# Hybrid diffusion step: a reordered opening, norm transposes at other places, and retention heads 1 to 3 written out

## What is computed

```python
def adaln(cvec, w, b):
    m = jax.nn.silu(cvec) @ w + b
    return jnp.split(m, N_MOD, axis=-1)      # shift, scale, gate; shift, scale, gate

def modulate(x, g, shift, scale):
    return rmsnorm(x, g) * (1.0 + scale) + shift

for l in range(DEPTH):
    mc, ml = adaln(c_ctx, ada_w[l], ada_b[l]), adaln(c, ada_w[l], ada_b[l])
    hc, hl = modulate(xc, norm_mix[l], ...), modulate(xl, norm_mix[l], ...)
    # l = 0: q, k, v, two gates = h @ weights; per head a forward and a backward scan over
    #        chunks of 128 tokens with decay exp(log_gamma * distance); y @ wo
    # l = 1: grouped-query attention, window 128, with a sink; y @ wo
    xc, xl = xc + mc[2] * yc, xl + ml[2] * yl
    hc, hl = modulate(xc, norm_ffn[l], ...), modulate(xl, norm_ffn[l], ...)
    # a = h @ w_in; depthwise conv of width 3; silu(g) * u; @ w_out
    xc, xl = xc + mc[5] * ffn(hc), xl + ml[5] * ffn(hl)
```

## Time and profile before

| | |
|---|---|
| median of 3 runs | 2097.97 us |
| the profiled execution, its whole time | 2103.55 us |
| its span, first to last instruction | 2101.7 us |
| mean granted TensorE clock | 0.985 |
| PE busy | 2016.7 us, 96% of the span |
| POOL, DVE, ACT busy | 752.6, 964.2, 662.9 us |
| DMA | 194.06 MB, mean 92 GB/s |

### The profile page before, as it was taken

One profiled execution on the slowest core, in us unless ns is written; L12 is line 12 of the kernel. 1 busy time (PEld: TensorE's weight loads), 2 busy tenths in 40 slices (PEclk: granted clock), 3 DMA queues, 4 the chain that ended last, 5 costly groups with the idle time before them and its releaser, 6 DMA issues.

```text
span 2101.7 us, 29771 instructions
## 1 busy us (share of the span) xinstructions
PE 2016.7 (96%) x11176; PEld 1680.7 (80%) x11176; DVE 964.2 (46%) x1281; ACT 662.9 (32%) x1323; POOL 752.6 (36%) x519
## 2 busy tenths in 40 slices
PE   6799999999999999999999999998979999999998
PEld 3685878588677847998898898895558998998996
DVE  2312420350133035753564475656624673575475
ACT  5332222222221234332233133425534332232232
POOL 3233233233323324433233333437844433333332
PEclk9999999999999999999999999998989999999999
DMA  7422332223223212342343222420002422222221
GB/s 296 177 71 70 102 118 71 77 93 102 77 91 110 70 50 98 113 150 70 120 140 111 70 73 77 171 78 16 1 11 91 151 72 79 70 80 73 77 71 51
DMA packets 53117, 194.06 MB, mean 92 GB/s; under 512 B 5920, under 2 KB 7328, under 8 KB 52000
## 3 DMA queue, kind: packets, MB, share of 16 engines
q1 hardware_dynamic: 48096, 174.68, 25.3%
q10 hardware_dynamic: 4928, 18.08, 2.2%
HBM read 185.65 MB, written 7.08 MB: 92 GB/s over the span
## 4 chain that ended last, share of the span: by engine, by line
PE 88%; issue 3%; ACT 3%; DVE 2%; POOL 2%; DMA 1%; DVEq 1%; POOLq 0%; ACTq 0%
PE ps L420 35%; PE ps L463 21%; PE ps L435 16%; PE ps L637 2%; PE ps L482 2%; PE ps L374 2%; PE ps L646 1%; ACT pr L1146 1%; PE ps L632 1%; POOL pr L1296 1%; PE ps L378 1%; PE ps L391 1%; PE ps L796 1%; PE ps L502 1%; PE ps L510 1%
## 5 line engine op out<-in xcount | busy, mean ns | idle before, releaser
L1190 POOL TENSOR_TENSOR w_l<-raw,w_h 128x1024 fp32r<-128x1024 f32 x232 | 564.7, 2436 | 1117.0 <-ACT w_h L845 1117.0
L420 PE MATMUL ps<-h_h,w_h 128*128 128x384 f32 (+1 forms) x1696 | 530.1, 313 | 2.7 <-issue 2.7
L420 PE MATMUL ps<-h_h,w_l 128*128 128x384 f32 (+1 forms) x1696 | 523.7, 309 | 0.0
L420 PE MATMUL ps<-h_l,w_h 128*128 128x384 f32 (+1 forms) x1696 | 523.6, 309 | 0.0
L845 ACT CAST w_h<-raw 128x1024 fp32r<-128x1024 f32 x232 | 245.3, 1059 | 559.0 <-PE ps L463 296.2
L420 PEld LDWEIGHTS ps<-h_h,w_h 128*128 128x128 f32 x1696 | 322.0, 190 | 16.2 <-issue 15.2
L420 PEld LDWEIGHTS ps<-h_l,w_h 128*128 128x128 f32 x1696 | 322.0, 190 | 2.6 <-issue 2.4
L420 PEld LDWEIGHTS ps<-h_h,w_l 128*128 128x128 f32 x1696 | 321.7, 190 | 0.0
L1562 DVE SCALAR_TENSOR_TENSOR cc<-ca,vec,cc 128x641 f32<-128x641 f32 x88 | 222.7, 2530 | 13.6 <-issue 12.4
L435 PE MATMUL ps<-w_h,h_h 128*128 128x512 f32 (+1 forms) x520 | 199.8, 384 | 1.0 <-issue 1.0
L435 PE MATMUL ps<-w_l,h_h 128*128 128x512 f32 (+1 forms) x520 | 198.2, 381 | 0.0
(11 more groups left out here) (190 smaller groups left out, 2670.9 us busy)
## 6 DMA issues: line engine op xcount, KB each, us to landing
raw<-stream_dram SPq DMA_DIRECT2D x312, 512.0 KB, 3.6
first_w<-first_dram SPq DMA_DIRECT2D x16, 512.0 KB, 15.6
gate<-gate_b_dram ACTq DMA_DIRECT2D x4, 1024.0 KB, 5.0
S<-state_dram ACTq DMA_DIRECT2D x4, 1024.0 KB, 7.4
new_state_dram<-st_out ACTq DMA_DIRECT2D x8, 512.0 KB, 3.1
xt<-x_dram ACTq DMA_DIRECT2D x5, 512.0 KB, 10.0
y_dram<-front SPq DMA_DIRECT2D x5, 512.0 KB, 2.6
rope_t<-rope_t_dram ACTq DMA_DIRECT2D x1, 512.0 KB, 9.1
```

The lines of the kernel that those rows point to most:

```text
L420: mm = nc.tensor.matmul(ps[:, banks + half, 0:width(half)], w, x[:, k, lo_hi(half)], start=(k == 0 and n == 0), stop=(k == KT - 1 and n == 2))
L1190: nc.gpsimd.tensor_tensor(w_l[:, r, :], raw[:, s, :], w_h[:, r, :].bitcast(F32), ALU.subtract).then_inc(raw_used[s], 1)
```

## The change

There are four edits.

1. **Small loads and the gate turn.** `gate` and the three table loads are issued from ACT in the middle of the opening, `rope_t` at its end without anything ahead of it. The exponentials move from ahead of the first evacuation to behind the evacuations of tiles 1 and 2; DVE's product with `tri` moves to behind the rotary work of q and k. DVE's wait for `rope_t` moves from ahead of the gate's copy to behind `gate_add`.
2. **Third modulation group.** `ada_first(2)` moves ahead of the transposes of token tiles 3 and 4, DVE's copy of it into the middle of `norm_f`, and the turns of groups 2 and 3 stand apart from their `ada_first`. `h_l` of token tile 4, half 0, is made by POOL.
3. **Norm transposes** in `first_tiles`: tile 3 after 2 steps k instead of 5, tile 4 after 6 instead of 8. Tile 4's second half of `norm_f` goes from ACT to DVE, its `h_l` half 0 from DVE to POOL, and ACT's `ada_copy` behind tile 3.
4. **Heads 1 to 3** are written out by a Python loop on the four engines. The condition in `hi` follows, since the head number is now a plain integer.

```diff
-POOL_LO = (0, 1, 3)
-            return t in (1, 3) if n == 0 else t >= 3 and hk == 1
+            return t in (1, 3) if n == 0 else (t, hk) == (3, 1)
+        def lo_on_pool(t, hk):
+            return t in (0, 1, 3) or (t, hk) == (4, 0)
@@ PE, first_tiles
-                first_pair(b, n, 0, range(0, 5))
+                first_pair(b, n, 0, range(0, 2))
                 norm_turn(n, 3)
-                first_pair(b, n, 0, range(5, KT))
+                first_pair(b, n, 0, range(2, 6))
                 norm_turn(n, 4)
+                first_pair(b, n, 0, range(6, KT))
@@ PE, opening
             ada_turn(0, 2)
+            ada_first(2)
             for t in range(3, TT):
                 norm_turn(0, t, (0,))
                 first_pair(b, 0, 0, range(0, 4))
-                ada_first(2)
-                first_pair(b, 0, 1, range(0, 2))
                 ada_turn(0, 3)
-                first_pair(b, 0, 1, range(2, 4))
+                first_pair(b, 0, 1, range(0, 1))
                 ada_first(3)
+                first_pair(b, 0, 1, range(1, 3))
                 ada_turn(0, 4)
+                first_pair(b, 0, 1, range(3, 4))
@@ PE, ACT, POOL, DVE
-            with pe.Fori(1, HEADS) as h:
+            for h in range(1, HEADS):
                 head(SEG["ret"], h, False)
@@ ACT, hi
-                if not (b.m0 + j < RING and isinstance(i, int)):
+                if not isinstance(i, int) or b.done(j, i) > RING:
@@ ACT, out_act
+                norm_f(n, 3, 1)
+                for hk in range(2):
+                    norm_hi(n, 3, hk)
                 ada_copy(SEG[NEXT_OF[n]], 0, 0, 3)
-                for t in (3, 4):
-                    norm_f(n, t, 1)
-                    for hk in range(2):
-                        norm_hi(n, t, hk)
+                for hk in range(2):
+                    norm_hi(n, 4, hk)
@@ ACT, opening and first head
                 if hk == 0:
                     hi(b0, 2, 0)
                     hi(b0, 3, 0)
-            act.dma_start(diff, dr["diff"]).then_inc(dec_in, 16)
-            ...
-            decay_tables(0)
-            decay_tables(1)
-            nc.scalar.activation(small[:, 56:64], small[:, 40:48], ACT.Exp, scale=float(P)).then_inc(dec_exp, 1)
-            act.dma_start(gate[:], dr["gate_b"][0]).then_inc(gate_in, 16)
+                    act.dma_start(gate[:], dr["gate_b"][0]).then_inc(gate_in, 16)
+                    act.dma_start(diff, dr["diff"]).then_inc(dec_in, 16)
+                    ...
             act.dma_start(rope_t[:], dr["rope_t"]).then_inc(rope_in, 16)
                     hi(b, j + RING, h)
+                    if first_head and j in (1, 2):
+                        decay_tables(j - 1)
@@ POOL, out_pool
                     norm_lo(n, 3, hk)
+                norm_lo(n, 4, 0)
@@ DVE, residual_norm
-                for hk in range(2):
-                    norm_lo(n, 4, hk)
+                norm_lo(n, 4, 1)
@@ DVE, opening and first head
             for t in range(TT):
                 norm_f(0, t, 0)
-            for t in (2, 4):
-                norm_lo(0, t, 0)
-            for n in range(2, 4):
-                ada_copy(None, n, 0, 0)
-                ada_mods(0, n + 1, FIRST[n])
+                if t == 2:
+                    ada_copy(None, 2, 0, 0)
+            norm_lo(0, 2, 0)
+            ada_mods(0, 3, FIRST[2])
+            ada_copy(None, 3, 0, 0)
+            ada_mods(0, 4, FIRST[3])
-                if first_head:
-                    dve.wait_ge(rope_in, 16)
                 ada_copy(b, 0, h, 0)
                     gate_add(0, adas + 1, 0, slice(0, 512))
+                if first_head:
+                    dve.wait_ge(rope_in, 16)
```

More of the change, by code:

```diff
@@ L312, in wait_lo @@
             for done, on_pool in ((hlo_pool, True), (hlo_dve, False)):
-                mine = [x for x in halves(n) if (x[0] in POOL_LO) == on_pool]
+                mine = [x for x in halves(n) if lo_on_pool(*x) == on_pool]
                 need = max((k + 1 for k, x in enumerate(mine) if x[0] in ts and x[1] == hk), default=0)
@@ L931, in decay_tables @@
             def decay_tables(d):
+                act.wait_ge(dec_lg, 1)
+                act.wait_ge(dec_in, 48)
                 for h in range(HEADS):
@@ L951, in _ @@
                     hi(b0, 3, 0)
-            act.dma_start(diff, dr["diff"]).then_inc(dec_in, 16)
[L953 to L956, removed]
-            decay_tables(0)
-            decay_tables(1)
-            nc.scalar.activation(small[:, 56:64], small[:, 40:48], ACT.Exp, scale=float(P)).then_inc(dec_exp, 1)
-            act.dma_start(gate[:], dr["gate_b"][0]).then_inc(gate_in, 16)
+                    act.dma_start(gate[:], dr["gate_b"][0]).then_inc(gate_in, 16)
+                    act.dma_start(diff, dr["diff"]).then_inc(dec_in, 16)
+                    act.dma_start(iota, dr["iota"]).then_inc(dec_in, 16)
+                    act.dma_start(tri, dr["tri"]).then_inc(dec_in, 16)
             act.dma_start(rope_t[:], dr["rope_t"]).then_inc(rope_in, 16)
@@ L974, in head @@
                     hi(b, j + RING, h)
+                    if first_head and j in (1, 2):
+                        decay_tables(j - 1)
+                    if first_head and j == 2:
+                        nc.scalar.activation(small[:, 56:64], small[:, 40:48], ACT.Exp,
+                                             scale=float(P)).then_inc(dec_exp, 1)
                     if j == 0:
@@ L1037, in _ @@
             head(b0, 0, True)
-            with act.Fori(1, HEADS) as h:
+            for h in range(1, HEADS):
                 head(SEG["ret"], h, False)
@@ L1266, in _ @@
                 lo(SEG["ret0"], j, 0)
-            for t in POOL_LO:
+            for t in (0, 1, 3, 4):
                 norm_lo(0, t, 0)
@@ L1270, in _ @@
                 lo(SEG["ret0"], j, 0)
-            for t in POOL_LO:
+            for t in (0, 1, 3):
                 norm_lo(0, t, 1)
@@ L1275, in _ @@
             rms(0)
-            with pool.Fori(1, HEADS) as h:
+            for h in range(1, HEADS):
                 for j in range(20):
@@ L1450, in _ @@
                 norm_lo(0, t, 1)
-            dve.wait_ge(dec_exp, 1)
-            for d in range(2):
-                op = V.tensor_tensor(dm[:, d], dm[:, d], over(tri[:, d, :], HEADS), ALU.mult)
-            op.then_inc(dec_ready, 1)
             gch = small[:, 56:64].rearrange("p (d h) -> p d h", d=2)
@@ L1487, in head @@
                     residual(h - 1, b, 4, h, 4)
+                if first_head:
+                    dve.wait_ge(dec_exp, 1)
+                    for d in range(2):
+                        op = V.tensor_tensor(dm[:, d], dm[:, d], over(tri[:, d, :], HEADS), ALU.mult)
+                    op.then_inc(dec_ready, 1)
+                    dve.drain()
                 ada_copy(b, 4, h, 1)
@@ L1533, in _ @@
             head(SEG["ret0"], 0, True)
-            with dve.Fori(1, HEADS) as h:
+            for h in range(1, HEADS):
                 head(SEG["ret"], h, False)
```

## The result

| | before | after |
|---|---|---|
| median of the paired runs | 2097.15 us (4 runs) | 2077.94 us (4 runs) |
| profiled execution, span | 2101.7 us | 2076.3 us |
| PE busy | 2016.7 us | 2010.2 us |
| mean granted clock | 0.985 | 0.988 |

The ratio is 0.9909, with a 95% interval of 0.9896 to 0.9922: the change takes off 19.2 us (16.4 to 21.8). I forecast 25.2. The two spans differ by 25.4 us, almost exactly the forecast. So the question for the experiments was why a sum that fits the two profiles misses the two medians by 6 us.

The account below looks back on a forecast made before the run. PE was busy 2016.7 of 2101.7 us, so gains come only from its gaps or half-speed matmuls. Opening 14.1 + heads 4.4 + layer openings 6.7 = 25.2 us, taken from the median 2097.97: 2072.8 us, range 2066 to 2083.

Parts of the forecast that it names:

- 6.7 in sum: Edit 3, three later layer openings: earlier first remainder and full clock save 2.9, 2.5 and 1.35 us.
- all four covers: Opening, edit 1: gate's load, weight tiles 2 and 3 (evacuations of tiles 0 and 1) and ACT's tables should not become late.
- 2.0 us of the clock: Gate turn, edit 1: behind a 0.8 us pause its four matmuls run at full speed, 1.72 us against 3.74.
- forecast of 10.9: Opening, edit 1: 8.9 us less wait at the gate turn plus 2.0 us from full clock.
- 3.2 forecast: Opening, edit 2: third group fills PE's 2.21 us pause at full speed; ACT's second-half norm_f starts near 45, not 48.22.
- rival of 2.2 us: Opening, edit 2: third group and transposes at half speed delay the pairs up to 2.2 us; within covers failing, 0.15.
- The new end: Layer openings, edit 3: POOL's three h_l at 1.25 us each end at 831.3 in n = 1, setting the first remainder.
- split as forecast: Three layer openings, edit 3: the pause ahead of part 1 splits, in sum 1 us.
- term of 4.4 us: Start of head 3, edit 4: written-out heads remove a 2.70 us issue gap and 1.69 us of slower first tile.
- an accident of the profiled execution: Rival, head 3's start: issue gap is accidental or returns elsewhere, edit 4 gives 0, result 2077.2 us; chance 0.07.
- Both jumps: Rival, starts of heads 2 and 3: both back jumps cost in timed runs, edit 4 worth 8.8 us, result 2068.4; chance 0.14.
- slower by instruction loads: Rival, heads 2 and 3: 14 more instruction loads each stall PE 4.4 us, cost 62, result 2139 us; chance 0.03.

Follow-up runs that it names:

- experiment 12: Changed kernel with the loop over heads 1 to 3 back on TensorE (PE) alone; other engines stay written out: 2081.14 us, ratio 0.9923 to the kernel before.
- experiment 1: The kernel before, unchanged, profiled and timed again: 2096.42 us, ratio 0.9998.
- experiments 5 and 9: Kernel before with edit 1 alone: 2091.91 us; with only edit 1's loads and tables reordered, DVE's wait for rope_t left ahead of the copy: 2090.52 us.
- experiment 7: Changed kernel with the third modulation group back at its old place (edits 1, 3, 4): 2082.97 us, ratio 0.9931 to the kernel before.
- experiments 2 and 12: 2: changed kernel with the loop over heads 1 to 3 back on all four engines (edits 1, 2, 3), 2082.84 us; 12: loop back on PE alone, 2081.14 us.
- experiment 10: Kernel before with the third modulation group at its new place (edit 2 alone): 2093.86 us, ratio 0.9984.

## Why the prediction came out as it did

The forecast was 2072.8, the result 2077.94: inside the range, 5.1 us too low. By places, each in all profiles that bear on it (start of one landmark on PE to the next; a layer opening is first norm transpose to gate turn; experiment 12 counts in the first two rows only):

| place | forecast | first pair | profiles without the edit | with it | difference |
|---|---|---|---|---|---|
| opening, to the scores of head 0 | 14.1 | 14.9 | 119.9 (4, 118.6 to 122.1) | 106.9 (4, 106.4 to 107.3) | 13.0 |
| three layer openings, each | 6.7 in sum | 6.4 | 29.1 (21, 28.5 to 30.2) | 27.4 (21, 27.3 to 27.7) | 1.66, 5.0 in sum |
| scores of head 2 to those of head 3 | 4.4 | 4.2 | 188.45 (8: five at 186.85, three at 191.0 to 191.2) | 187.0 (5) | 1.45 |
| scores of head 0 to those of head 2 | 0 | -0.4 | 373.75 (8) | 374.4 (5) | -0.6 |
| gate turn of n = 1 to the first transposes of n = 2 | 0 | 1.35 | 469.1 (8, 468.2 to 470.3) | 467.5 (5, 467.3 to 467.8) | 1.6 |

The sum is 13.0 + 5.0 + 1.45 - 0.6 + 1.6 = 20.4 us, against 19.2 measured (16.4 to 21.8). Two more stretches scatter over the fourteen profiles without a clear tie to an edit: from the scores of head 3 to the first transposes of n = 1 the first pair lost 3.35 us, from the gate turn of n = 2 to the transposes of n = 3 (266.4 to 269.1) it gained 2.1. With them, the first pair adds up to its 25.4.

**A gain that the prediction's sum lacks.** The last row of the table lies behind the heads, in the first FFN, and goes with edit 4: no profile with a loop on PE is as short as the longest of the five written out. The other matmuls of that stretch take 454.0 us in all fourteen profiles. The difference is in the seven `ada_block`, whose 16 matmuls use a weight chunk raw: their sum, each to the start of what follows, is 13.3 to 13.8 us written out and 14.2 to 16.5 else, with experiment 12 (loop on PE alone, 470.5 for the stretch) at the upper end. Two of the seven in the changed kernel, the same two in experiment 1, and the longest in experiment 12 (timelines of PE):

```profile
1028.06 1.92 PE L486 MATMUL ps<-raw,csil 128*32 128x512 f32 x16
1059.14 1.92 PE L486 MATMUL ps<-raw,csil 128*32 128x512 f32 x16
```

```profile
1042.74 2.20 PE L482 MATMUL ps<-raw,csil 128*32 128x512 f32 x16
1074.10 2.19 PE L482 MATMUL ps<-raw,csil 128*32 128x512 f32 x16
```

```profile
997.71 1.91 PE L487 MATMUL ps<-raw,csil 128*32 128x512 f32 x12
1000.43 1.05 PE L487 MATMUL ps<-raw,csil 128*32 128x512 f32 x4 [0.81 <-DMA raw<-stream_dram]
```

The last row names the chunk's load. Why it lands earlier where the heads are written out is not shown.

**Edit 1, right.** The wait was on `rope_t`, the copy follows in 0.84, and all four covers held: tile 2 starts at 59.48, no wait on `qk_evac` appears, `gate_add` and the tables cost nothing. The size went with the load: in the four profiles without edits 1 and 2 `rope_t` landed 9.1, 7.7, 6.8 and 6.7 us after its issue, and the pause was 9.69, 7.93, 6.61 and 6.60; issued ahead of the tables it landed in 3.4 to 3.6 us, in all eight profiles that have it so. The 2.0 us of the clock were 1.75 (from the gate turn to the scores of head 0 it is 50.90 in the first profile, 49.15 in the changed kernel): I took 3.74 from a timeline and 1.72 from the chain, and in a timeline the same four matmuls at full speed are 1.88. In two profiles (experiments 5 and 9) the opening is 8.0 us shorter (111.9); in a third without edit 2 (experiment 7, 108.78) it is 11.1, near the forecast of 10.9. Of the 3.1 us between them 1.5 are the half speed behind POOL's pause; before that, the first pairs ran at half speed for longer (`norm_f` of the second half at 47.15 and 46.94, against 45.45).

**Edit 2, right in place, too large.** 3.2 forecast, 2.0 and 1.9 in the profiles. I took full speed, "because the pause that would let the clock fall is the one that is filled"; that was the failed step of this term. The group's matmuls take 3.2 to 4.9 us in all six profiles with the edit, and there are two reasons. In four profiles (the changed kernel's two, experiments 2 and 12) PE is at the group at 25.1 to 25.8 us, before its weights: PE's weight loads wait 2.7 or 2.8 us for the chunks, and the clock falls meanwhile (granted 0.50 to 0.54 from 26.5 to 29.5 us in the first). In experiment 10 PE comes there at 29.5 and waits for no chunk, but all 16 run at half speed (1.06 us each and not 0.59), 3.64 us in sum. I had that as a rival of 2.2 us; it cost 1.3, as the pairs behind it run at full speed again. ACT's `norm_f` came 4.3 us earlier than in the profile before, but only 1.5 to 2.3 earlier (43.1 to 43.9) than in experiment 7. The rest goes with the clock: the second group took 3.64 us in the profile before, and 1.92 in the one after.

**Edit 3, right.** The new end is POOL's third `h_l`, 1.5 us behind ACT's cast of that tile, and the pauses are split as forecast, in sum 0.8 us in n = 1, 0.7 in n = 2 and 1.2 in n = 3. The gain per place has two parts: 1.15 us always (28.55 to 27.4), and 1.55 where the clock would have fallen, which it did in 7 of 21 places without the edit and in none of 21 with it. I counted the second part in two of three places, as the first profile had it.

**Edit 4 and the step that failed.** The term of 4.4 us was read rightly from the earlier trace rows, and it is in 3 of 8 profiles with loops and in 0 of 5 written out. In each of the three the page has 66 instruction packets, in the other five 57, and in the five written-out ones 70. So the gap comes in executions that load nine packets more, and three of them land around it. I still read it as code of the loop body that is loaded again, but that is argued: the view names no engine for these packets, though the prediction puts them on PE's queue. I had "an accident of the profiled execution" as a rival with 0.07. What failed is the sentence "that execution is 5.6 us above the median of the runs, without a stage that I can blame; I carry the difference over". The stages to blame were the terms of my own sum: the gap (4.4 against an execution without it), the long wait on `rope_t` (the opening stood 2.2 above the mean of four) and one more half-speed opening than usual (1.5), less 2.4 of luck behind head 3. Whoever removes what made an execution slow must subtract it from that execution's time: 2103.55 - 25.2 = 2078.35 us, 0.4 from the result. That it comes so near is partly luck: the 3.35 us lost behind head 3 and the 1.35 and 2.1 us gained later in the first pair are none of my terms, and they cancel.

The Trainium skill (Runtime: NRT & Kernel Launch, Instruction fetch mechanics) says that a taken branch outside the prefetched window stalls until its code is fetched. By that, each back jump out of the window would cost; in eight profiles the jump to head 2 never did, and the one to head 3 did in the three where instruction packets appear at it. "Both jumps" and "slower by instruction loads" are refuted: the straight code loads 13 packets more than a loop without the gap, and no new issue pause over 0.73 us appears.

## What to carry to other kernels

A stall in one profile is a term only after it has been seen in a second one; where the profiled execution stands above the median, first suspect the terms that you are about to subtract, and subtract from that execution's own time. When a wait holds an engine that others need, look at what issued the transfer and what is queued ahead of it: moving the loads and tables was worth all of edit 1, moving the wait alone less (a pause of 4.05 us stayed, against 0.84), because the next thing in the queue (the product on the tables) was late too. Work for a pause must need neither the bank nor the data that the pause is for.

## What the runs showed of the hardware

- The kernel before loaded 66 packets of instructions in one execution and 57 in the next. Of the nine profiles with a loop on PE three have 66 and six have 57, and TensorE stalls 2.4 to 2.7 us at head 3, with part of the tile behind it at half speed, only in those with 66.
- Behind the same pauses the granted clock falls to 1.2 GHz in some executions and stays at 2.4 in others: behind 1.27 us in the opening, it fell in 3 of 14 profiles; behind the 2.25 us wait of `first_pair`, in 7 of 21; behind head 3, at pauses of 2.0 and 0.6 to 1.1 us, in 11 of 14. In the layer openings with edit 3, with a pause of 0.35 and one of 0.37 to 0.84 us, it fell in none of 21. At the gate turn it fell in all six profiles with a pause of 4.05 to 9.69 us, and in none of the eight with 0.84 or 0.92.
- The written-out scan shows an issue pause of 0.7 us once per head (four, against one for the loop), 2.9 us in sum; between the scores of heads 0 and 2 the written-out kernels take 0.6 us more in the mean (0.3 to 1.4).
- A load of 512 KB (`rope_t`) took 6.0 to 9.1 us from issue to landing where it was issued behind the exponentials, at 59 to 61 us (six profiles), and 3.4 to 3.6 us where it was issued at 47 to 51 us (eight profiles).
